# Feed-forward input products by seven quadrant products over 256 tokens, on one Trainium2 core

## What is computed

```python
def swiglu_ffn(x, w_in, w_out):
    gate, up = jnp.split(x @ w_in, 2, axis=-1)
    return (jax.nn.silu(gate) * up) @ w_out

h = h + 0.5 * swiglu_ffn(rmsnorm(h, gain), w_in, w_out)   # four times
```

## Time and profile before

| | |
|---|---|
| median of 3 runs | 2215.12 us (2214.97 to 2216.24) |
| span of the profiled execution | 2213.7 us |
| TensorE busy | 2198.3 us (99%), 10012 matmuls |
| VectorE busy | 1071.2 us (48%) |
| ScalarE busy | 748.3 us (34%) |
| GpSimd busy | 439.2 us (20%) |
| chain that ended last | TensorE 97%, issue 1% |
| DMA | 213.54 MB, 96 GB/s on average |

### The profile page before, as it was taken

One profiled execution on the slowest core, in us unless ns is written; L12 is line 12 of the kernel. 1 busy time (PEld: TensorE's weight loads), 2 busy tenths in 40 slices (PEclk: granted clock), 3 DMA queues, 4 the chain that ended last, 5 costly groups with the idle time before them and its releaser, 6 DMA issues.

```text
span 2213.7 us, 26476 instructions
## 1 busy us (share of the span) xinstructions
PE 2198.3 (99%) x10012; PEld 1820.3 (82%) x10012; DVE 1071.2 (48%) x1126; ACT 748.3 (34%) x1000; POOL 439.2 (20%) x343
## 2 busy tenths in 40 slices
PE   8999999999999999999999999999999999999998
PEld 6888888888777888888888888888788888888887
DVE  6444334453466545444444544443588866444322
ACT  5232222232233334222232422223472354232222
POOL 1222101620123002222211222230002003222101
PEclk9999999999999999999999999999999999999999
DMA  4322234333222232233333223233322123233232
GB/s 147 95 97 101 95 105 133 95 115 100 81 79 74 87 99 99 96 95 95 95 107 111 92 99 95 95 105 105 110 71 67 53 82 95 95 99 100 95 105 96
DMA packets 60255, 213.54 MB, mean 96 GB/s; under 512 B 6688, under 2 KB 9120, under 8 KB 59936
## 3 DMA queue, kind: packets, MB, share of 16 engines
q1 hardware_dynamic: 59616, 209.50, 29.5%
q0 software_dynamic: 288, 2.62, 0.3%
q10 hardware_dynamic: 288, 0.52, 0.1%
HBM read 210.52 MB, written 2.10 MB: 96 GB/s over the span
## 4 chain that ended last, share of the span: by engine, by line
PE 97%; issue 1%; DVE 0%; DMA 0%; POOL 0%; ACT 0%; SPq 0%; POOLq 0%
PE acc L541 30%; PE acc L543 30%; PE acc L542 30%; PE mixb L1022 1%; PE mixb L1045 1%; PE acc L984 1%; PE acc L983 1%; PE acc L982 1%; PE mixb L867 0%; PE acc L878 0%; PE mixb L878 0%; DMA w_raw<-weights 0%; PE acc L867 0%; PE sums L788 0%; PE sums L592 0%
## 5 line engine op out<-in xcount | busy, mean ns | idle before, releaser
L541 PE MATMUL acc<-x_hi,w_hi 128*128 128x512 f32 x2016 | 792.7, 393 | 7.8 <-DVE x_lo L1528 7.8
L543 PE MATMUL acc<-x_hi,w_lo 128*128 128x512 f32 x2016 | 786.0, 390 | 0.0
L542 PE MATMUL acc<-x_lo,w_hi 128*128 128x512 f32 x2016 | 785.7, 390 | 0.0
L541 PEld LDWEIGHTS acc<-x_hi,w_hi 128*128 128x128 f32 x2016 | 379.2, 188 | 86.7 <-DVE x_lo L1528 8.8
L543 PEld LDWEIGHTS acc<-x_hi,w_lo 128*128 128x128 f32 x2016 | 379.0, 188 | 79.7
L542 PEld LDWEIGHTS acc<-x_lo,w_hi 128*128 128x128 f32 x2016 | 379.4, 188 | 77.5
L1509 DVE TENSOR_TENSOR w_lo<-w_raw,w_hi 128x1024 fp32r<-128x1024 f32 x231 | 298.0, 1296 | 232.7 <-ACT w_hi L1095 231.7
L1621 DVE TENSOR_TENSOR w_lo<-w_raw,w_hi 128x1024 fp32r<-128x1024 f32 x160 | 246.3, 1539 | 271.0 <-ACT w_hi L1101 271.0
L1095 ACT ACTIVATE w_hi<-w_raw 128x1024 fp32r<-128x1024 f32 x231 | 242.1, 1054 | 286.6 <-DMA w_raw<-weights 286.6
L541 PE MATMUL acc<-hid_hi,w_hi 128*128 128x512 f32 (+1 forms) x726 | 277.9, 383 | 0.0
L542 PE MATMUL acc<-hid_lo,w_hi 128*128 128x512 f32 (+1 forms) x726 | 277.7, 383 | 0.0
(11 more groups left out here) (363 smaller groups left out, 1749.7 us busy)
## 6 DMA issues: line engine op xcount, KB each, us to landing
w_raw<-weights SPq DMA_DIRECT2D x391, 512.0 KB, 3.4
y_t<-h SPq DMA_DIRECT2D x16, 128.0 KB, 1.8
h<-x_t SPq DMA_DIRECT2D x3, 512.0 KB, 6.8
k1c<-const POOLq DMA_DIRECT2D x1, 1536.0 KB, 9.2
k2c<-const POOLq DMA_DIRECT2D x1, 1024.0 KB, 7.8
h<-x_t ACTq DMA_DIRECT2D x2, 256.0 KB, 4.0
w_raw<-weights SPq DMA_DIRECT2D x1, 384.0 KB, 5.2
cst<-const SPq DMA_DIRECT2D x1, 161.0 KB, 8.4
```

The source lines that it names most:

```text
L541: pe.matmul(bank, w_hi[:, slot, w], hi, start=start, stop=False)
L542: pe.matmul(bank, w_hi[:, slot, w], lo, start=False, stop=False)
L543: return pe.matmul(bank, w_lo[:, slot, w], hi, start=False, stop=stop)
```

## The change

Let a double be two neighbouring 128-column tiles of gate and the two tiles of up that belong to them: four weight blocks, 32 products of 128 x 512 tokens before. The change computes a double as a 2 x 2 block product. The weights' quadrants are a11, a21, a22 and a12, each one block of 128 x 1024; the other factor's quadrants are the even and the odd tiles of x, for the first (t1) and the second (t2) 256 tokens. Seven products (p1, p6, p2, p7, p5, p4, p3 in order of execution, each a block of 8 products of 128 x 256) give all four results. It is the Winograd form of Strassen's algorithm. In each of the 4 feed-forward stages there are 11 doubles.

- VectorE forms four sums of weight blocks for each double (s3, s2, s4, s1; `weight_sum`, line 1713 of the changed kernel), since three of the seven blocks are loaded and four are sums in the order used here.
- ScalarE and VectorE form combinations of x: `xc_hi` and `xc_lo` hold for each pair of tiles seven versions (B11, B21, B22, T2, U3, U1, U4) of 256 tokens (`combine`, `round_mixed`, `mix_halves`, `mixed_rest`).
- The banks are read by seven VectorE instructions of 2 x 256 elements for each double (`quad`); ScalarE copies p1 to f_s. silu is one instruction of 1024 elements for each double, and so are hid_f, hid_hi and hid_lo; hid_f and hid_lo are on VectorE (lines 1878 and 1883), and GpSimd has no part left in the input stages. rstd is applied to gate before silu; for up it is applied when a tile is added to h, by one more VectorE instruction of 512 elements (`add_tile`, lines 1810 and 1815).
- The inner width 2816 is taken in two passes: 6 doubles, then output tiles over 12 tiles of hid, then 5 doubles, then output tiles over 10. h is added to in each pass.
- Raw blocks and residues share eight buffers whose use is planned by a table (`RAW`, `LO`, `LOADS`, `FREED`); SyncE's loads wait for the block that frees their buffer. The loops are written out.
- At the program's start the first weight block is loaded and split whole; x comes in four parts. The final tail is ordered differently (`TAIL_ACT`, `last_tile`).

```diff
+PRODUCTS = ("p1", "p6", "p2", "p7", "p5", "p4", "p3")
+COMBO = (B11, T2, B21, U3, U1, U4, B22)
+HALVES = (6, 5)
...
+            def quadrants(f, d, n0, before, fresh):
...
+                    opens = i in (P1, P6, P5)
+                    for u in range(2):
+                        for k in range(KD // 2):
...
+                            last = product(n, 4 * u + k, bank[:, u, :], xc_hi[:, k, x, :], xc_lo[:, k, x, :],
+                                           opens and k == 0, k == KD // 2 - 1, read_between=True)
+                    last.then_inc(block_done, 1)
+                    if d % sum(HALVES) == 0 and i == NORM_AT[f]:
+                        split_sum(f"norm{FFN_NORM[f]}")
...
+            def weight_sum(d, name):
...
+                out, one, two = (w_raw[RAW[UNIT0[d] + i]][:, :] for i in (out, one, two))
+                dve.tensor_tensor(out, one, two, ALU.add).then_inc(w_summed, 1)
...
+            def mix_halves(r, j):
...
+                dve.tensor_tensor(xc_f[:, j, U3, :], xc_f[:, j, U1, :], xc_f[:, j, U3, :], ALU.subtract).then_inc(x_mixed, 1)
+                dve.wait_ge(x_mixed, 12 * f + 3 * j + 1)
+                dve.scalar_tensor_tensor(xc_f[:, j, T2, :], h[:, 2 * j, t1], even, xc_f[:, j, U3, :], ALU.mult,
+                                         ALU.subtract).then_inc(x_mixed, 1)
+                dve.scalar_tensor_tensor(xc_f[:, j, U1, :], h[:, 2 * j, t1], even, xc_f[:, j, U1, :], ALU.mult, ALU.subtract)
+                dve.wait_ge(x_mixed, 12 * f + 3 * j + 2)
+                dve.scalar_tensor_tensor(xc_f[:, j, U4, :], h[:, 2 * j + 1, t1], odd, xc_f[:, j, T2, :], ALU.mult,
+                                         ALU.subtract).then_inc(x_mixed, 1)
...
+                        before(n0 + P2)
+                        if not fresh:
+                            hidden(d - 1)
+                        split(n0 + P2)
...
+                        prepare(n0 + P7)
...
+                        dve.tensor_tensor(f_gate[:, :, t2], r_b, f_s[:, :, :], ALU.subtract).then_inc(quad, 1)
+                        prepare(n0 + P5)
+                        if begin:
+                            inverse_root()
+                        if not (begin and f == 2):
+                            gate_first()
+                        prepare(n0 + P4)
...
+                        prepare(n0 + P3)
...
+                        prepare(n0 + 7)
...
+                        prepare(n0 + 8)
```

More of the change, by code:

```diff
@@ new lines, with doubles @@
+FACTOR = {"w_ab": 1, "g": 2, "e_q": 3, "keys": 4}
+NDOUBLE = 4 * sum(HALVES)
+def doubles(f, p):
+    first = sum(HALVES) * f + (HALVES[0] if p else 0)
+    return [(first + d, FIRST[f"ffn{f}_in{p}"] + 7 * d) for d in range(HALVES[p])]
+UNIT0 = dict(d for f in range(4) for p in range(2) for d in doubles(f, p))
+DOUBLE_AT = {n0 + i: (d, i) for d, n0 in UNIT0.items() for i in range(7)}
+OUT_SEQ, OUT_END = [], []
+for _p in range(2):
+    _nk = 2 * HALVES[_p]
+    _early = _nk - 2
+    _seq = [(m, k) for m in range(2) for k in range(_early)] + [(m, k) for m in range(2) for k in range(_early, _nk)]
+    _seq += [(m, k) for m in range(2, 8) for k in range(_nk)]
+    OUT_SEQ.append(_seq)
+    OUT_END.append([max(g for g, mk in enumerate(_seq) if mk[0] == m) for m in range(8)])
@@ new lines, with tile_end, _take @@
+TILE_ENDS = [[m for m in range(8) if OUT_END[p][m] % 8 != 7] for p in range(2)]
+def tile_end(f, p, m):
+    g = OUT_END[p][m]
+    if g % 8 == 7:
+        return "block", FIRST[f"ffn{f}_out{p}"] + g // 8 + 1
+    return "tile", f * (len(TILE_ENDS[0]) + len(TILE_ENDS[1])) + (len(TILE_ENDS[0]) if p else 0) + TILE_ENDS[p].index(m) + 1
+BUFFERS = 8
+RAW, LO, LOADS, LOADED, FREED = {}, {}, [], {}, {}
+_free = {slot: -1 for slot in range(BUFFERS)}
+_times = {slot: 0 for slot in range(BUFFERS)}
+def _take(name, load, slots=BUFFERS):
+    slot = min(range(slots), key=lambda s: (_free[s], s))
+    if load:
+        LOADS.append((slot, _free[slot]))
+        _times[slot] += 1
+        LOADED[name] = (slot, _times[slot])
+    else:
+        FREED[name] = _free[slot]
+    after, _free[slot] = _free[slot], NB
+    return slot
@@ L651, in last_sum @@
+            def ffn(f):
+                for p in range(2):
+                    for i, (d, n0) in enumerate(doubles(f, p)):
+                        quadrants(f, d, n0, OUT0[f"ffn{f}_in{p}"], i == 0)
+                    out_tiles(f, p)
             def last_sum(t):
@@ new lines, in chain, with add_tile @@
+            def chain(m):
+                dve.wait_ge(sq_done, KD * 3 + m + 1)
+                dve.tensor_scalar(h[:, m, :], h[:, m, :], vcol("norm_final", m), None, ALU.mult).then_inc(chained, 1)
+            def add_tile(f, p, m):
+                out0 = OUT0[f"ffn{f}_out{p}"]
+                end, value = tile_end(f, p, m)
+                dve.wait_ge(END[end], value)
+                dve.scalar_tensor_tensor(f_tmp[:, m % 2, :], acc[m % 4], 0.5, rstd[:, :], ALU.mult,
+                                         ALU.mult).then_inc(drained, 1)
+                if f == 2 and p == 0 and m == 0:
+                    dve.wait_ge(h_final, KD)
+                dve.wait_ge(drained, out0 + m + 1)
+                dve.tensor_tensor(h[:, m, :], h[:, m, :], f_tmp[:, m % 2, :], ALU.add).then_inc(h_added, 1)
@@ L2392 @@
     arrays = {
-        "weights": np.concatenate(list(_weights(v))).reshape(NB, P, TILES * P),
+        "weights": np.concatenate([w.reshape(-1, P, TILES * P) for w in _weights(v)]),
         "x_t": np.ascontiguousarray(v["x"][0].T.reshape(KD, P, S).transpose(1, 0, 2)),
```

869 lines of the change are left out of this document (511 added, 358 removed), and 3 rows, old and new, of the table PHASES.

## The result

The changed kernel takes **2239.45 us** (median of 4 runs, 2239.0 to 2239.9) where the kernel before takes 2215.3 beside it: a ratio of 1.0109, interval 1.0095 to 1.0123. It is slower by 24 us; the prediction said 2192 and faster.

The account below looks back on a forecast made before the run. TensorE, busy 99% of the span, was taken as the bound: 2213.7 - 70.4 (doubles) + 25 + 3 + 11 + 7.5 (starts) + 1 (end) = 2190.8, plus 1.4 for the median: 2192 us, range 2165 to 2222.

Parts of the forecast that it names:

- TensorE's gain: Input stages: a double falls from 21.76 to 20.16 us, so 44 doubles take 70.4 us off TensorE's queue.
- VectorE's load and the steady state at nothing: Input-stage doubles: VectorE needs 18.9 us of 20.16, plus 0.3 for dependent instructions, adding nothing to TensorE's time.
- (a): Rival, chance 0.15: VectorE bounds the input stages, a double needs 20.9 us, doubles save only 38 us, total 2224.
- (c): Rival, chance 0.07: TensorE's waits show at each 128x256 block, 308 blocks cost 31 us, total 2223.
- (b): Rival, chance 0.13: the stage starts cost less, 20 us, total 2165.
- (d): Rival, chance 0.03: the full gain with starts costing as before, total 2145.
- Program's start: First double of the program: VectorE's queue delays p2 to 38.7 and p4 to 50.4 us, losing 25 us.
- Second feed-forward, 3 us: Start of the second feed-forward: p2 starts at 8.7 instead of 6.2, p4 waits 0.7 more; 3 us lost.
- Combinations keep pace with mixer tiles of 5.4 us: Tiles before the second feed-forward: VectorE's combinations of x keep up with TensorE's mixer tiles of 5.4 us.
- Third feed-forward, 11 us: Start of the third feed-forward: late p6, second norm's sum, two reciprocals and p2's own delay lose 11 us.
- The chain through norm_final's multiplication: Third feed-forward's start: one more square and scaling a tile delay p6 by 2 us.
- Fourth and end, 8.5 us: Fourth feed-forward's start loses 7.5 us, VectorE needing 29 us beside mixer tiles of 21.8; the program's end loses net 1.

Follow-up runs that it names:

- narrow additions: GpSimd's additions of the squares work on 8 of 512 columns: in the changed kernel 2214.9 us; in the kernel before 2214.5 us.
- fourth edit: Third feed-forward's product of h with the norm's factor moved from GpSimd to VectorE, added to the three edits on the changed kernel: 2194.3 us, ratio 0.9906.
- roundings ahead: Changed kernel with ScalarE's weight roundings one block further ahead in the tiles that end a stage: 2229.5 us, ratio 1.0064.
- three edits: Changed kernel with rounded squares summed by TensorE, ScalarE's weight roundings one block ahead and the first norm's sum on TensorE: 2198.0 us, ratio 0.9924.
- staged start: Changed kernel with the first norm's sum on TensorE and start combinations in the order products want them: 2240.4 us; with squares made early, 2233.3 us.

## Why the prediction was wrong

**TensorE's gain: right.** 44 doubles less 1.60 us; every undisturbed double takes 20.16.

**VectorE's load and the steady state at nothing: right**, and the runs with one and two instructions more confirm the 18.9 us and the 0.3 beside it: doubles of 20.4 and 21.7 where the sums are 20.4 and 21.6. Rivals (a) and (c) fall: no double of 20.7, no gap at blocks. (b) and (d) fall with the starts, which cost more and not less.

**Program's start: right.** 25 us predicted, 27.8 found; p2 at 40.7 (predicted 38.7), p4 at 53.3 (50.4). It was the one start that was put on paper instruction by instruction, and the one without GpSimd.

**Second feed-forward, 3 us: wrong, 13.1** (0.6 in the mixer, 3.3 in its last tiles, 9.2 in the first double, each against the kernel before). The step is "Combinations keep pace with mixer tiles of 5.4 us". It used the pair's 4.4 us from the program's start, with two readings (1.2) and two splits (2.3) some 7.9 us of 10.88 (the instructions come to about 7.6 in the trace). The trace has 11.84. Missing were L1760's 1.0 and a split's 0.25 beside GpSimd, and 2.98 us of waiting for ScalarE, whose list I had only summed up (10 us a double) and never ordered. At the program's start next to nothing of both shows: GpSimd is idle, and only p1's rounding of weights stands between. So the price was taken from a place where the other user of it was absent, though the trace before showed the pattern: the splits take 1.54 us in the input stages, "GpSimd being at work there". I used that row only to take the cost out where GpSimd left, not to put it in where GpSimd stayed.

The Trainium skill (SBUF — State Buffer, "Who interferes with whom") has the rule: a VectorE instruction with two SBUF inputs contends with a GpSimd instruction that reads SBUF, and so can `tensor_scalar` in its two-port modes; the first to start holds the port for its whole length and the other blocks. The trace agrees: L1760 and GpSimd's addition above, and L1803 at 1522 ns against 577 with narrow additions. The readings of banks, with one input in SBUF, keep their 0.68.

**Third feed-forward, 11 us: wrong, 35.0** (10.8 of them in the second output pass of the second). The step is "The chain through norm_final's multiplication (one more square and scaling a tile) delays p6 by 2": p6 starts 8.5 us after p1 where it needs 2.9. There GpSimd adds two squares a tile and VectorE has the additional L1803, so a pair takes 19 to 20 us where TensorE needs 13.6, and not only the last tile is late but the whole pass from 1198 us on. With narrow additions the pass falls from 65.2 to 56.1. In the first double, the reciprocals were counted, GpSimd's product of h beside them was not (4 us, the fourth edit).

**Fourth and end, 8.5 us: 18.0.** The 29 us of VectorE in 21.8 of TensorE was the right mechanism, but too small. GpSimd's additions are 5.3 of it (26.2 and 33.7 us against 24.1 and 30.5 in the table); ScalarE's order is not, as the roundings ahead gain nothing there (27.2 and 34.0). The remaining 4 us or so stay open.

So of 47 us missed, GpSimd's additions account for 24.5, shown by leaving them out of the changed kernel and, with no effect, of the kernel before. Its product of h accounts for about 4 (3.7, on top of the three edits), the order of ScalarE's list for up to 10, though these overlap. The rest is not divided further: the parts of the reciprocals, of the norm's rest and of the clock in it weren't tried one by one in the changed kernel. The 0.13 that I gave to "slower" stood on rivals (a) and (c), a bound steady state and waits at blocks, and neither happened. The slower time came from the starts, whose uncertainty I had set at a third, from the same rows as the value itself; no rival let them cost more.

## What to carry to other kernels

A price per instruction is good only with the same neighbours: before it is carried to another place, look in the timeline at what GpSimd and the partner engine do beside it there, and put the partner's list in order too, not only its sum. When a change moves work onto an engine that was half idle, list what its idle time had been hiding; that cost was in the kernel before, where its total time shows nothing of it and only the durations of single instructions do. A gain in the steady state is earned once per double and paid back once per start, so the start of each stage deserves the same instruction by instruction working as the steady state.

## What the runs showed of the hardware

GpSimd and VectorE blocked each other in both directions. In the run with narrow additions an addition of 8 columns takes 0.29 us alone, and 1.17 beside a VectorE instruction, with an end just after that one's (GpSimd, then VectorE):

```profile
849.95 0.29 POOL L2507 TENSOR_TENSOR sumsq<-sumsq,square 128x8 f32<-128x8 f32 x1 [4.28 <-ACT square L1259]
856.03 1.17 POOL L2507 TENSOR_TENSOR sumsq<-sumsq,square 128x8 f32<-128x8 f32 x1 [5.79 <-ACT square L1259]
```
```profile
855.92 1.22 DVE L1713 TENSOR_TENSOR w_raw<-w_raw 128x1024 f32<-128x1024 f32 x1
```

It can chain. In the changed kernel a weight sum held GpSimd's addition up, and the addition then held the next split up, which took 2.31 us in place of 1.22:

```profile
858.05 1.22 DVE L1713 TENSOR_TENSOR w_raw<-w_raw 128x1024 f32<-128x1024 f32 x1
859.18 2.31 DVE L1725 TENSOR_TENSOR w_lo<-w_raw,w_hi 128x1024 fp32r<-128x1024 f32 x1
```
```profile
858.14 2.27 POOL L2507 TENSOR_TENSOR sumsq<-sumsq,square 128x512 f32<-128x512 f32 x1 [5.73 <-ACT square L1259]
```

A blocked instruction counts as busy, so no idle time and no releaser shows it. What shows it is one shape with two durations. And a ones matrix in full float32 cost TensorE 0.86 us a tile of 512 (four records in 1.88 us for two squares, their starts 0.43 apart), against 0.227 for rounded operands. In the waits of the first product it was free all the same: with it p6 starts 18.7 us after p1, as without. Put behind later products, in the staged start, it was what ScalarE waited for.
